# Rotary queries of the latent heads: the halves exchanged by vector-engine reads 32 partitions apart instead of by a product with a permutation matrix

## The reference

```python
q_m = (_rmsnorm(c_q, q_norm) @ w_uq).reshape(B, T, MLA_HEADS, QK_HEAD)
q_m = jnp.concatenate([q_m[..., :QK_NOPE], _rope(q_m[..., QK_NOPE:], qpos)], axis=-1)
...
def _rope(x, pos):
    ...
    x1, x2 = xf[..., :half], xf[..., half:]
    return jnp.concatenate([x1 * cos - x2 * sin, x1 * sin + x2 * cos], axis=-1)
```

## Time and profile before

| | |
|---|---|
| time, median of 3 runs | 2364.78 us (2364.59 to 2365.21) |
| time of the profiled execution | 2364.43 us |
| its span, first to last instruction | 2362.1 us |
| TensorE busy | 2353.3 us |
| VectorE busy | 1187.2 us |
| ScalarE busy | 808.9 us |
| granted TensorE clock, mean | 1.000 |

### The profile page before, as it was taken

One profiled execution on the slowest core, in us unless ns is written; L12 is line 12 of the kernel. 1 busy time (PEld: TensorE's weight loads), 2 busy tenths in 40 slices (PEclk: granted clock), 3 DMA queues, 4 the chain that ended last, 5 costly groups with the idle time before them and its releaser, 6 DMA issues.

```text
span 2362.1 us, 36463 instructions
## 1 busy us (share of the span) xinstructions
PE 2353.3 (100%) x16057; PEld 2331.4 (99%) x16057; DVE 1187.2 (50%) x945; ACT 808.9 (34%) x719; POOL 123.2 (5%) x64
## 2 busy tenths in 40 slices
PE   9999999999999999999999999999999999999998
PEld 9999999999999999999999899999999999999998
DVE  6444444444444446656695456434444444444445
ACT  6232232232322224353543444323232232232324
POOL 1000000000000000000100001000000000000000
PEclk9999999999999999999999999999999999999999
DMA  7444444444444444535345134444444444444442
GB/s 258 144 159 143 148 154 142 156 146 145 156 142 153 149 144 151 186 112 178 104 138 167 53 127 159 145 149 153 142 156 146 145 157 142 153 149 144 158 142 81
DMA packets 194665, 347.01 MB, mean 147 GB/s; under 512 B 10858, under 2 KB 35952, under 8 KB 194608
## 3 DMA queue, kind: packets, MB, share of 16 engines
q1 hardware_dynamic: 190912, 337.34, 43.9%
q0 software_dynamic: 2480, 7.63, 0.9%
q10 hardware_dynamic: 1216, 1.20, 0.2%
HBM read 340.50 MB, written 5.65 MB: 147 GB/s over the span
## 4 chain that ended last, share of the span: by engine, by line
PE 99%; DVE 1%; DMA 0%; issue 0%; ACT 0%; SPq 0%; ACTq 0%
PE ps L1626 31%; PE ps L1627 31%; PE ps L1628 31%; PE ps L1691 0%; PE ps L1694 0%; PE ps L1697 0%; PE ps L2036 0%; PE ps L2056 0%; PE ps L1756 0%; PE ps L2024 0%; PE ps L2196 0%; PE ps L1880 0%; PE ps L1874 0%; PE ps L1853 0%; PE ps L2037 0%; PE ps L1820 0%
## 5 line engine op out<-in xcount | busy, mean ns | idle before, releaser
L1626 PE MATMUL ps<-mov_hi,w_hi 128*128 128x320 f32 x3504 | 1087.0, 310 | 0.0
L1628 PE MATMUL ps<-mov_hi,w_lo 128*128 128x320 f32 x3504 | 1082.7, 309 | 0.0
L1627 PE MATMUL ps<-mov_lo,w_hi 128*128 128x320 f32 x3504 | 1082.7, 309 | 0.0
L1056 DVE TENSOR_TENSOR w_lo<-raw,w_hi 128x2048 fp32r<-128x2048 f32 x309 | 708.2, 2292 | 740.6 <-ACT w_hi L612 740.1
L612 ACT CAST w_hi<-raw 128x2048 fp32r<-128x2048 f32 x309 | 588.5, 1904 | 1417.1 <-PE ps L1628 1413.4
L1626 PEld LDWEIGHTS ps<-mov_hi,w_hi 128*128 128x128 f32 x3504 | 657.8, 188 | 1.3 <-issue 0.2
L1627 PEld LDWEIGHTS ps<-mov_lo,w_hi 128*128 128x128 f32 x3504 | 657.8, 188 | 0.6
L1628 PEld LDWEIGHTS ps<-mov_hi,w_lo 128*128 128x128 f32 x3504 | 657.7, 188 | 0.0
L1626 PE MATMUL ps<-h_hi,w_hi 128*128 128x320 f32 x1472 | 454.7, 309 | 0.0
L1628 PE MATMUL ps<-h_hi,w_lo 128*128 128x320 f32 x1472 | 454.4, 309 | 0.0
L1627 PE MATMUL ps<-h_lo,w_hi 128*128 128x320 f32 x1472 | 454.4, 309 | 0.0
(11 more groups left out here) (265 smaller groups left out, 832.1 us busy)
## 6 DMA issues: line engine op xcount, KB each, us to landing
raw<-in_ffn_w_up SPq DMA_DIRECT2D x88, 1024.0 KB, 5.2
raw<-in_ffn_w_down SPq DMA_DIRECT2D x88, 1024.0 KB, 5.0
raw<-in_ffn_w_gate SPq DMA_DIRECT2D x86, 1024.0 KB, 5.1
raw<-in_w_in SPq DMA_DIRECT2D x28, 1024.0 KB, 5.4
raw<-in_w_out SPq DMA_DIRECT2D x16, 1024.0 KB, 5.1
raw<-in_mla_w_uq SPq DMA_DIRECT2D x12, 256.0 KB, 4.0
raw<-in_w_in SPq DMA_DIRECT2D x4, 640.0 KB, 4.1
work<-in_x_prompt SPq DMA_DIRECT2D x8, 256.0 KB, 6.4
```

Of the source, the lines that this page charges most:

```text
L1056: dve.tensor_tensor(w_lo[:, n % SPLIT_SLOTS, :], raw[:, n % RAW_SLOTS, :], w_hi[:, n % SPLIT_SLOTS, :].bitcast(F32), ALU.subtract).then_in ...
L1626: pe.matmul(out, w[0], x[0], start=first, stop=False)
L1627: pe.matmul(out, w[0], x[1], start=False, stop=False)
L1628: return pe.matmul(out, w[1], x[0], start=False, stop=last)
```

## The change

The product with `swap` for the queries goes, and with it the wait on TensorE for the copied queries. Instead DVE multiplies UQ0's accumulators by the sine table in four operations of 32 partitions each. Each reads the block of 32 partitions next to the one that it writes. `q ^ 1` is the neighbouring block's number. The cosine product now reads the accumulators too, in place of the copy, and it is what reports UQ0 as drained. The two pairs of 32-partition operations stand on either side of the weight split `next_lo(U_UQ + 1)`, which makes UQ2's `w_lo`. The splits that stood at the head of each step now stand at the end of the one before. The number `GR_ROPE` stays as a group number with no products: DVE's addition counts it as drained.

```diff
-            for j in range(3):
-                next_lo(U_UQ + j)
+            def rope_swapped(q):
+
+                to, of = slice(32 * q, 32 * q + 32), slice(32 * (q ^ 1), 32 * (q ^ 1) + 32)
+                dve.tensor_tensor(wk3(M_RT, 4, T, to), bank4(GR_UQ)[of], over(sin[to], 4), ALU.mult)
+
+            next_lo(U_UQ)
+            dve.wait_ge(unit_used, U_UQ + 1)
+            rope_swapped(0)
+            rope_swapped(1)
+            next_lo(U_UQ + 1)
+            rope_swapped(2)
+            rope_swapped(3)
+            dve.tensor_tensor(wk3(M_QR, 4, T), bank4(GR_UQ), over(cos, 4), ALU.mult).then_inc(drained, 1)
+            for j in (1, 2):
                 dve.wait_ge(unit_used, U_UQ + j + 1)
-                dve.tensor_copy(wk3((M_QR, M_QN, M_QN + 4 * T)[j], 4, T), bank4(GR_UQ + j)).then_inc(drained, 1)
-            next_lo(U_OA2)
+                dve.tensor_copy(wk3(M_QN + 4 * T * (j - 1), 4, T), bank4(GR_UQ + j)).then_inc(drained, 1)
+                next_lo(U_UQ + j + 1)
             dve.wait_ge(o_lo_done, 2)
             dve.memset(wk(M_CTNEW, KVL, slice(DEC, P)), 0.0).then_inc(pad_zero, 1)
             link(dve.memset(wk(M_QRD, 4 * P), 0.0))
-            dve.wait_ge(swap_ready, 2)
-            dve.tensor_tensor(wk3(M_RT, 4, T), bank4(GR_ROPE), over(sin, 4), ALU.mult).then_inc(drained, 1)
-            link(dve.tensor_tensor(wk3(M_QR, 4, T), wk3(M_QR, 4, T), over(cos, 4), ALU.mult))
+            dve.wait_ge(drained, GR_ROPE)
+            dve.tensor_tensor(wk(M_QR, 4 * T), wk(M_QR, 4 * T), wk(M_RT, 4 * T), ALU.add).then_inc(drained, 1)
             dve.wait_ge(drained, GR_ROPE + 1)
-            link(dve.tensor_tensor(wk(M_QR, 4 * T), wk(M_QR, 4 * T), wk(M_RT, 4 * T), ALU.add))
...
-            pe.wait_ge(drained, GR_UQ + 2)
-            for a in range(4):
-                ins = pe.matmul(bank4(GR_ROPE)[:, a, :], swap, wk(M_QR + T * a, T), start=True, stop=True)
-            ins.then_inc(swap_ready, 1)
```

## The result

The changed kernel takes 2369.28 us (median of 19 runs, 2367.26 to 2370.64). The kernel before takes 2364.59 us (19 runs, 2364.19 to 2365.81). The ratio is 1.0019, with a 95% interval of 1.0012 to 1.0025. So it is 4.7 us slower, where I forecast 2.7 us, and it lies 0.3 us above the top of my range. The runs also spread more: 3.4 us, where the kernel before has 1.6 here (2.5 and 2.25 us in its 33 and 25 later runs).

A forecast was written before the change was run, and what follows sets the result against it. TensorE was taken to bound the kernel; 2.97 us of idle before UQ2 less 0.27 us gained before OA2 gave +2.70 us on 2364.78, so 2367.5 us, range 2366.2 to 2369.0.

The forecast's parts named there:

- TensorE is the bound, nothing later swallows or adds: Whole kernel: TensorE busy 2353.3 of 2362.1 us, so whatever its line of work gains or loses goes to the end.
- The removed product gives 0.27 of its 2.15 us: Between UQ2 and OA2: OA2 must wait for UQ2's copy, so only 0.27 us of the product's 2.15 are gained.
- The four operations take 1.49 us each: VectorE after UQ0: each 32-partition operation takes as long as a 128-partition one, 1.49 us, bounds 0.37 to 3.0.
- my two steps: Start of one VectorE exchange operation to the next: 1.41 us without a wait, 1.52 us if held for the one before.
- UQ2 is held by UQ0's drain for 2.97 us: In front of UQ2: UQ0 drained at about 1265.3, so TensorE idles 2.97 us (2.69 to 3.21).
- my sum: +2.97 us in front of UQ2, −0.27 us in front of OA2: +2.70 us (2.42 to 2.94).
- The clock stays at 1.00: Throughout, including the 3 us gap before UQ2: the granted clock would not fall.
- a rival with 3 in 100: Clock falls to 1.2 GHz in the gap for all of UQ2, its 7.04 us doubling: 2374.5 us; chance 0.03.
- The signs: Wrong if a 32-partition operation takes under 0.75 or over 2.0 us, or TensorE starts UQ2 without waiting.
- Within 0.2%: Whole kernel: a difference under 0.2%, 4.7 us, counts as no change; chance 0.91.
- The range: Whole kernel time: 2366.2 to 2369.0 us, from the runs' spread, operation lengths and later release of TensorE.

The follow-up runs named there:

- copy_first: Changed kernel, but UQ0 copied to SBUF at once, that copy reporting it drained, and the exchange made from the copy: 2364.62 us, kernel before 2364.72.
- by_each_tile: As copy_first, but UQ2 copied tile by tile, OA2 waiting for each tile only before its own tile in the same bank: 2362.76 us, kernel before 2364.64.
- held_drain: Kernel before, exchange product kept, plus four 128-partition VectorE multiplications without crossing between UQ0's end and its copy: 2369.56 us, kernel before 2364.64.
- five: Changed kernel with the fourth exchange operation done twice, to lengthen the gap before UQ2 from 3.0 to 4.5 us: 2371.34 us, kernel before 2364.64.

## Why the prediction was wrong, point by point

- *TensorE is the bound, nothing later swallows or adds.* Right. The stretch's 5.62 us are the span's 5.7.
- *The removed product gives 0.27 of its 2.15 us, since OA2 waits for UQ2's copy.* Right. In the execution without a change of clock, OA2's second product starts 0.23 us earlier behind UQ2's last than before (2.21 us in place of 2.44). copy_first gives 0.24 by itself, and by_each_tile gives the rest once that wait is taken away.
- *The four operations take 1.49 us each.* Right: 2.98 and 3.00 us for the pairs. They went near the upper of my two steps: the second starts 1.50 us after the first, while L1540 starts 1.41 us after L1537 and 0.08 us before its end. The Trainium skill says in "VectorE: DVE Perf Modes", section "Two Vector instructions with no wait between them", that an instruction whose input starts in another block of 32 partitions than the last one's from that memory waits until all earlier ones have finished, and the trace agrees.
- *UQ2 is held by UQ0's drain for 2.97 us.* Right in kind, 0.2 us short. The drain ended at 1265.54, the upper end of my estimate, TensorE's weight load came 0.12 us later, not 0.05, and the step from the first product to the second takes 0.22 us, not 0.15. Without a change of clock both gaps, less the removed product, cost 2.96 us, where my sum had 2.70 (2.42 to 2.94).
- *The clock stays at 1.00.* This is the step that failed. I had it as a rival with 3 in 100 and left its price out of the range. I judged it by one row, the idle end of the kernel, where the clock stayed up for 3 us and more. From that single fall I took that a gap of 3 us is too short. That fall, after 4.8 us, was a late one: the ends of the ten profiles have it after 2.1 to 5.2 us. The runs show that a gap of 3 us is long enough in most executions: only 3 of 19 lie under 2368 us, near the 2367.6 that the gap alone gives (2364.59 + 2.96). The median lies 1.7 us above that. I had priced the rival for a whole unit, 7.04 us more; it costs 2.65 us in the profiled execution, as only 21 steps went at the lower level, each for 0.12 us more and not for the 0.147 of a doubling.
- *The signs.* I named three signs of being wrong, and none of them came up; the clock wasn't among the three.
- *Within 0.2%.* Right at 0.19%, but partly by luck: my sum left the clock out, and 1.7 us more still fitted under the bound of 4.7 us.
- *The range.* Its top, 2369.0, was made of small uncertainties of the operations' length. Half of the clock's price would have covered the result.

The mechanism, the place and the order of the waits were as forecast. 2.96 of the 4.69 us are the gaps less the removed product, and about 1.7 are what the clock adds to them in the median.

## What to carry to other kernels

Work taken from the busiest engine is worth only what isn't waiting behind it: look which drain or copy the removed work was covering, here 1.9 of 2.15 us. When an accumulator gets more readers, find the report that frees it and count up everything in the queue before it. And price a gap on TensorE of some 3 us not by its length alone: here the clock added over half of it again in the median run, and a few products whose result nobody reads, put into the gap, cost less than leaving it empty. One trace isn't enough to tell at what length a gap becomes dear: the same program lost 2.65 us in one execution and nothing in another.

## What the runs showed of the hardware

- A gap can bring the granted clock down, but its length alone doesn't decide it. With 1.5 us of idle in front of UQ2 none of 11 runs shows a sign of it. With 3.0 us the same program lost 0 and 2.65 us in two profiled executions. With 4.5 us all nine runs lie 1.4 us or more above what the gaps give, though a part of that can come from outside the stretch; the one profiled lost 1.5 us there. At the ends of the ten profiles the clock falls after 2.1 to 5.2 us of idle. In its Part 1, on the clock gate, "TensorE: Matmul & The Clock Gate" of the Trainium skill says that TensorE's activity sets the clock and that idleness halves it; the traces agree, with products 0.267 us apart in place of 0.147 at 0.50.
- The clock can fall after the gap. In held_drain TensorE worked for 1.4 us at full pace behind the gap of 2.9 us before it fell, and in five it fell as work began again. Why it does so in one execution and not in the next, these runs don't settle.
- Product steps at the lower level are 1.8 times as long as at the upper (0.267 and 0.147 us).
- A VectorE operation that reads 32 partitions and writes the 32 beside them takes as long as one on 128 with no crossing: 1.48 to 1.50 us for 1280 columns in each case, from PSUM and from SBUF.
